# A weight ring of 20 slots in place of 18, each slot over the work region filled when its last reader is done

## The chip, the core and the metric

The kernel runs on one core of a Trainium2 chip. The metric is the device time of one execution in microseconds (us); lower is better. PE is the matrix engine, DVE the vector engine, ACT the scalar engine, POOL the general one, SP the engine whose queue issues most loads. 16 DMA engines serve the core.

## What is computed

Two layers of a model over 256 prompt tokens and 32 sample tokens (8 sequences of 4), D = 1024, all in 32-bit floats. Layer 0 has the even mixer (attention with forget gates, with paged keys and values for the samples, beside a gated delta rule), layer 1 the odd mixer (a gated product along chunks). Behind each mixer stands a mixture of 32 experts, of which each token takes two of one group:

```python
for layer in range(DEPTH):
    hp, hs = rms_norm(xp, norm_mix[layer]), rms_norm(xs, norm_mix[layer])
    ...                                    # even_mixer or odd_mixer gives mp, ms
    xp, xs = xp + mp, xs + ms
    xp = xp + hier_moe(rms_norm(xp, norm_ffn[layer]), *mprm)
    xs = xs + hier_moe(rms_norm(xs, norm_ffn[layer]), *mprm)

def hier_moe(h, w_rg, w_re, w_gate, w_up, w_down):
    ...                                    # group by argmax, two experts in it, softmax weights: gates
    act = silu(hg) * hu * gates[..., None] # hg, hu: h times w_gate[e], w_up[e], 1024 x 256 each
    return einsum('nlef,efd->nld', act, w_down)
```

The outputs are the rows behind the last norm, the new keys, values and gates, and the states; among these the samples' delta states (`delta_sample`, 2 MB).

## The kernel before

**The expert stage.** The experts are worked through in 8 turns (NQ) of 4 experts (QE). In a turn q, PE gathers the rows of its experts (`gather`, L1382, a product with a selection `pl`), multiplies them by gates and ups (`gate_up`, L1396; in turn 0 and 7 `gate_part`, L1415), transposes the activations (`act_turn`, L1436), multiplies by the downs (`down`, L1449; `down_last` in three parts, L1466) and adds the rows back in the next turn (`out_rows`, L1498 and L1507). ACT takes the silu (L2028, into `sg`), copies the transposes (L2033, into `avT`) and half of the products (L2041, into `ysb`), and a part of the gathered rows (`rows_in`, L2019, into `xgT`); DVE does the other parts (L2633, L2710, L2732), the additions to x (L2641, L2647), and in turn 0 the rare swap of a crowded expert (`swap`, L2573 to L2593, which ends with `meta_rdy`). The general case, in which an expert has more rows than fit, is a loop behind a branch that every engine takes at turn SPLIT = NQ - 2 = 6; it isn't entered with these inputs.

**The weights.** A unit is a gate, an up or a down of one expert, 1 MB. A layer has 96 units; unit u goes into slot u % RSLOTS of a ring, by one DMA on SP's queue (L487). `first_loads` issues the units from RSLOTS on, each when the unit that was in its slot before has been read (`first_free`: `part_ps` for the four gates of turn 0, then `gu_ps` and `dn_ps`). The ups and downs of the last turn come in pieces (L532, L526). Slots 0 to 7 (SLOTS) also hold the weights of the two mixers, one after another. Slots 8 and up lie over the work region of the mixers (`wk(offset)`: slot 8 + offset // 2048): in the even mixer for instance `S0`, the sample states, lies in slots 8 and 9, and in the odd mixer `vrow` in 8 to 10, `urow` in 11 to 13, the norm's weights in 14 and 15, `uT` from 17 on. Behind the ring lie 5240 columns that hold the router's and the expert stage's own tiles (`rt`, `pwT`, `spb`, `av`, `avT`, `ysb`, `cnt`).

**The order on SP's queue.** SP works strictly in order. At the end of a mixer it loads units 0 to 7, each as soon as the mixer's weights in its slot have been read (`even_used`, `odd_used`), then it waits for the end of the mixer and for all stores, and loads the others:

```python
sp.wait_ge(s.x_new, 6 * layer + 3)
sp.wait_ge(s.out_misc, 16 * (13 + layer))
for u in range(SLOTS, RSLOTS):
    moe_load(layer, 0, u)
first_loads(layer)
```

`x_new` counts the additions of the mixer's output to x (L2502, L2507), `out_misc` the stores, that of the samples' states (L1998, issued on ACT's queue when `dl_su` is 8) among them. The first expert stage is followed by the loads of the odd mixer's first 8 weights (`odd_first`), the second by the last norm's weight (`nfw`, slot 12).

**The router.** Before a stage PE transposes x in 8 pieces k (`transpose_k`, L812), ACT and DVE copy them to `hT`, and PE adds the product of each piece with the router's weights (L1340) two pieces behind the transposes; then come the choice of experts on DVE and the first gather.

## Time and profile before

| | |
|---|---|
| runs shown | 1065.19, 1061.83 and 1065.3 us, median 1065.19 us |
| profiled execution | 1060.95 us, its span 1059.0 us |
| busy in the span | PE 90%, PE's weight loads 54%, DVE 40%, ACT 22%, POOL 8% |
| matrix engine's granted clock | 0.972 of full speed in the mean |
| DMA | 292.63 MB, 276 GB/s in the mean; SP's queue 267.63 MB of it |

The span runs from the first to the last instruction; the execution's own time is 1.95 us longer. A share of busy time is a mean over stages with different limits: what sets the length of a stage is read from the waits in it and from what its DMA does meanwhile. The two expert stages lie at about 365 to 602 us and 813 to 1050 us.

### The profile page before, as it was taken

The numbers are of one execution on the slowest core, as the hardware profiler recorded it, in microseconds if no ns is written. First come the engines' busy times: TensorE is split into PE (matmuls) and PEld (weight loads), VectorE is DVE, ScalarE is ACT, GpSimd is POOL, SyncE is SP. The second block draws the span as 40 slices with busy tenths as digits, with TensorE's granted clock in tenths as the row PEclk, the third lists the DMA queues.
The fourth block names the chain that finished last, engine by engine and source line by source line (L and its number), as shares of the span: only waits on it lengthen the run. The fifth ranks groups of instructions, "written<-read, shape, count | busy, mean of one in ns | idle before, by whom it ended". The sixth has DMA issues, their size and how long they took to land.

```text
span 1059.0 us, 18436 instructions
## 1 busy us (share of the span) xinstructions
PE 957.5 (90%) x6934; PEld 576.6 (54%) x6934; DVE 424.1 (40%) x1105; ACT 237.8 (22%) x513; POOL 88.5 (8%) x199
## 2 busy tenths in 40 slices
PE   8999989899989999977788899999999999777885
PEld 7777767586884374533453444444444755333532
DVE  3733455465744346322534200252002553224343
ACT  3321136354201141110110311331002411010102
POOL 6333242140000000000000000000000000000000
PEclk9999999999979999988999999999999999899999
DMA  9951178795602599999999964443335899999995
GB/s 288 254 172 37 42 244 261 268 355 214 225 1 83 183 384 414 420 421 421 420 419 414 352 233 159 159 159 119 130 119 185 358 417 420 421 421 421 417 414 207
DMA packets 93391, 292.63 MB, mean 276 GB/s; under 512 B 16355, under 2 KB 56859, under 8 KB 66382
## 3 DMA queue, kind: packets, MB, share of 16 engines
q1 hardware_dynamic: 78836, 267.63, 66.1%
q0 software_dynamic: 5152, 17.05, 5.1%
q10 hardware_dynamic: 9306, 6.67, 2.0%
q8 instruction: 59, 0.97, 0.4%
q14 instruction: 38, 0.31, 0.1%
HBM read 286.17 MB, written 5.16 MB: 275 GB/s over the span
## 4 chain that ended last, share of the span: by engine, by line
PE 72%; DMA 15%; DVE 5%; SPq 3%; issue 3%; ACT 2%; ACTq 0%; DVEq 0%
DMA arena<-in_moe_w_up 13%; PE ps L1659 10%; PE ps L914 10%; PE ps L1396 8%; PE ps L1382 5%; PE ps L1749 5%; PE ps L1028 3%; PE ps L838 2%; DMA arena<-in_moe_w_down 2%; PE ps L1449 2%; PE ps L1041 2%; PE ps L829 2%; PE ps L1415 1%; PE ps L858 1%; PE ps L1652 1%
## 5 line engine op out<-in xcount | busy, mean ns | idle before, releaser
L1396 PE MATMUL ps<-arena,hT 128*32 128x512 f32 x768 | 95.6, 655 | 33.5 <-DMA arena<-in_moe_w_up 33.5
L1659 PE MATMUL ps<-arena,hT 128*128 128x512 f32 x256 | 111.0, 593 | 0.0
L914 PE MATMUL ps<-hT,arena 128*128 128x288 f32 x448 | 110.0, 407 | 0.0
L1382 PE MATMUL ps<-lvl,htok 128*128 128x128 f32 (+1 forms) x768 | 97.2, 284 | 14.0 <-issue 7.1
L1382 PEld LDWEIGHTS ps<-lvl,htok 128*128 128x128 f32 x768 | 91.9, 194 | 23.2 <-issue 17.7
L914 PEld LDWEIGHTS ps<-hT,arena 128*128 128x128 f32 x448 | 84.6, 190 | 23.5 <-issue 0.5
L1659 PEld LDWEIGHTS ps<-arena,hT 128*128 128x128 f32 x256 | 48.3, 190 | 59.7 <-issue 59.4
L1396 PEld LDWEIGHTS ps<-arena,hT 128*32 128x32 f32 x768 | 27.8, 119 | 96.1 <-issue 96.1
L1507 PE MATMUL ps<-arena 128*128 128x512 f32 x112 | 55.2, 618 | 3.8 <-DVE x L2641 3.8
L2633 DVE TENSOR_SCALAR hT<-ps,nw 128x128 f32<-128x128 f32 (+1 forms) x64 | 22.6, 354 | 75.9 <-PE ps L1382 75.8
L1449 PE MATMUL ps<-arena 128*32 128x512 f32 x448 | 51.0, 595 | 1.3 <-ACT arena L2033 1.3
L1749 PE MATMUL ps<-arena 128*128 128x512 f32 x112 | 49.2, 592 | 0.0
L2710 DVE TENSOR_TENSOR arena<-ps,lfp 128x256 f32<-128x256 f32 x16 | 6.8, 423 | 97.1 <-ACT lfp L2028 97.1
L2019 ACT ACTIVATE hT<-ps,nw 128x128 f32<-128x128 f32 (+1 forms) x64 | 23.7, 371 | 94.8 <-PE ps L1382 94.8
L2028 ACT ACTIVATE lfp<-ps 128x256 f32<-128x256 f32 x16 | 6.1, 384 | 168.9 <-PE ps L1396 138.0
L779 POOL DMA_DIRECT2D arena<-in_cache_v x64 | 33.8, 528 | 82.9 <-PE ps L1117 35.7
L757 POOL DMA_DIRECT2D lfp<-in_cache_logf x64 | 34.5, 539 | 61.2 <-issue 61.2
L1507 PEld LDWEIGHTS ps<-arena 128*128 128x128 f32 x112 | 18.9, 188 | 34.2 <-DVE x L2641 15.0
L2647 DVE TENSOR_TENSOR x<-x,ps 128x512 f32<-128x512 f32 x56 | 36.0, 684 | 2.7 <-PE ps L1507 2.3
L1749 PEld LDWEIGHTS ps<-arena 128*128 128x128 f32 x112 | 20.7, 190 | 23.4 <-issue 23.4
L1028 PE MATMUL ps<-ident,arena 128*128 128x128 f32 x256 | 32.2, 276 | 1.1 <-DVE hT L2304 1.0
L2732 DVE COPY arena<-ps 128x512 f32<-128x512 f32 x14 | 9.7, 692 | 53.3 <-PE ps L1449 53.3
(495 smaller groups left out, 1303.0 us busy)
## 6 DMA issues: line engine op xcount, KB each, us to landing
arena<-in_moe_w_gate SPq DMA_DIRECT2D x64, 1024.0 KB, 20.6
arena<-in_moe_w_up SPq DMA_DIRECT2D x56, 1024.0 KB, 20.9
arena<-in_moe_w_down SPq DMA_DIRECT2D x56, 1024.0 KB, 21.4
arena<-in_cache_k SPq DMA_DIRECT2D x64, 256.0 KB, 4.0
arena<-in_cache_v POOLq DMA_DIRECT2D x64, 256.0 KB, 3.9
arena<-in_w_in_odd SPq DMA_DIRECT2D x16, 1024.0 KB, 10.5
arena<-in_w_in_even SPq DMA_DIRECT2D x14, 1024.0 KB, 9.1
arena<-in_moe_w_up SPq DMA_DIRECT2D x16, 512.0 KB, 9.0
```

The costliest lines, as they stand in the source:

```text
L757: pool.dma_start(lfp[:, grp, pg, bass.ds(bl * 8, 8)], cl[bass.ds(page, 1)].rearrange("a r h -> r (a h)")).then_inc(s.bias_pages, 16)
L779: pool.dma_start(vquad[gi:P:4, qd, bl].rearrange("p j c -> p (j c)"), cvp[bass.ds(page, 1)].rearrange("a (p j) h d -> (a p) (j h d)", j=4))\
L914: last = mm(ps[:, c % 4, 0:T], w[:, k, P * (c % 2):P * (c % 2 + 1)], hT[:, k, :], start=k == 0, stop=k == KD - 1)
L1028: last = tr(ps[:, kt_bank(n), P * c:P * (c + 1)], kbuf[t % 4][:, n % 4, P * c:P * (c + 1)], ident[:, :])
L1382: last = mm(ps[:, row_bank(k), 0:w], htok[:, i, P * k:P * (k + 1)], pl[:, i, 0:w], start=i == 0, stop=i == 2)
L1396: last = mm(ps[EC * j:EC * (j + 1), q % 2, :], xgT[q % 2][:, k, EC * j:EC * (j + 1)], ring[:, sl:sl + 2, DE * k:DE * (k + 1)], start=k == ...
L1449: last = mm(ps[EC * j:EC * (j + 1), 3 + hf, :], avT[:, q % 2, f, EC * j:EC * (j + 1)], w[:, f, 512 * hf:512 * (hf + 1)], start=f == 0, sto ...
L1507: mm(ps[:, row_bank(j), :], pwT[:, q % 2, P * i:P * (i + 1)], ysb[:, 512 * hf:512 * (hf + 1)], start=True, stop=True).then_inc(s.o_ps, 1)
L1659: last = mm(ps[:, bank, :], hT[:, k, P * i:P * (i + 1)], ring[:, oslot(2 * n):oslot(2 * n) + 2, QC * k:QC * (k + 1)], start=k == 0, stop=k ...
L1749: mm(ps[:, b, :], uT[:, c, P * (b // 2):P * (b // 2 + 1)], w[:, e, 512 * (b % 2):512 * (b % 2 + 1)], start=c == 0, stop=False)
L2019: A_(xgT[q % 2][:, k, 0:w], ps[:, row_bank(k), 0:w], ACT.Copy, scale=nw[:, n_, k:k + 1])\
L2647: V.tensor_tensor(xs, xs, ps[:, row_bank(j), :], ALU.add).then_inc(s.xadd, 1)
```

## The change

- RSLOTS is 20. The ring takes 4096 columns more, and the columns behind it shrink from 5240 to 1441: `spb`, `lgT` and one `pwT` stay there; `av`, `sg`, `avT`, `ysb`, `cnt` and the other `pwT` go to tiles that are idle in the expert stage, and `av`, `sg` and `avT` have one buffer in place of two. `rt` goes to the end of `hT`, under `xgT[1]`; what of it is needed later (`w1`, `w2`, `spq`) goes to `sm`, and ACT waits for `meta_rdy` before it writes `xgT[1]`.
- The slots over the work region are loaded by `fill_even` and `fill_odd`, each group when its last reader is done; 18 and 19 wait for the end of the mixer.
- The store of the samples' states has its own semaphore `s0_stored`; only slots 8 and 9, where they lie, wait for it.
- The branch is at turn SPLIT = 4.
- The router transposes two pieces and then multiplies two.
- Behind the first stage, SP loads the odd mixer's weights 0 to 3 when turn 6's downs have been read, and 4 to 7 when turn 7's gates and ups have been read.
- Some semaphores are merged (`fz_ln` and `dl_dtx` into `act_ln`, `rt_exp2` into `rl_sb`, `hot_dve` and `y_quarter` into `side_dve`).

The diff, cut to its core:

```diff
-MSLOTS, RSLOTS = 3 * QE, 18
+MSLOTS, RSLOTS = 3 * QE, 20
...
-        arena = sb("arena", [P, RSLOTS * UNIT + 5240])
+        arena = sb("arena", [P, RSLOTS * UNIT + 1441])
...
-        rt = wk(M, 3, 320)
-        pwT = wk(M + 1344, 2, T)
-        spb = wk(M + 1920, 4, T)
-        lgT = wk(M + 1920, 3 * P)
-        av = wk(M + 3072, 2, DE)
-        avT = wk(M + 3584, 2, FT, P)
-        ysb = wk(M + 4096, D)
-        cnt = wk(M + 5120, 112)
+        spb = wk(M, 4, T)
+        lgT = wk(M, 3 * P)
+        pwT = [wr[:, 0, :, :].rearrange("p k c -> p (k c)"), wk(M + 1152, T)]
+        av, sg = neg2, wsm[:, :, :].rearrange("p k c -> p (k c)")
+        ysb = [lfp[:, :, :, :].rearrange("p a b c -> p (a b c)"), cst[:, 1024:1536]]
+        cnt = cst[:, 320:432]
+        avT = cst[:, 432:432 + FT * P].rearrange("p (f c) -> p f c", f=FT)
         pw2 = cs27[:, :, :].rearrange("p c w -> p (c w)")[:, 0:T]
-        sg = lfp[:, :, :, :].rearrange("p a b c -> p (a b c)").rearrange("p (a b) -> p a b", a=2)
...
-        nfw = ring[:, 12, 0:D]
+        rt = xgf[:, KD * (P + EC) + 64:].rearrange("p (t c) -> p t c", t=3)
+        nfw = ring[:, 16, 0:D]
...
-        SPLIT = NQ - 2
+        SPLIT = NQ - 4
...
+
+            def fill_even():
+
+                def over_weights(*us):
+                    for u in us:
+                        even_used(EVEN_UNITS - SLOTS + (u - EVEN_UNITS) % SLOTS)
+                        moe_load(0, 0, u)
+
+                over_weights(2, 3, 4, 5)
+                sp.wait_ge(s.dl_oss_ps, 1)
+                sp.wait_ge(s.dl_vexp, NB)
+                for u in (14, 15, 16, 17):
+                    moe_load(0, 0, u)
+                over_weights(6, 7, 0)
+                sp.wait_ge(s.dl_su, 8)
+                for u in (10, 11, 12, 13):
+                    moe_load(0, 0, u)
+                over_weights(1)
+                sp.wait_ge(s.x_new, 3)
+                sp.wait_ge(s.out_misc, 16 * 12)
+                for u in range(18, RSLOTS):
+                    moe_load(0, 0, u)
+                sp.wait_ge(s.s0_stored, 16)
+                for u in (8, 9):
+                    moe_load(0, 0, u)
+
+            def fill_odd():
+
+                def over_weights(*us):
+                    for u in us:
+                        odd_used(ODD_UNITS - SLOTS + u)
+                        moe_load(1, 0, u)
+
+                sp.wait_ge(s.gm_sum, 6)
+                for u in (14, 15):
+                    moe_load(1, 0, u)
+                over_weights(0, 1, 2, 3)
+                moe_load(1, 0, 17)
+                over_weights(4)
+                sp.wait_ge(s.gm_m_ps, HC + 1)
+                moe_load(1, 0, 16)
+                sp.wait_ge(s.out_misc, 16 * 13)
+                for u in (8, 9, 10):
+                    moe_load(1, 0, u)
+                over_weights(5)
+                sp.wait_ge(s.gm_t_ps, NU)
+                for u in (11, 12, 13):
+                    moe_load(1, 0, u)
+                over_weights(6, 7)
+                sp.wait_ge(s.x_new, 9)
+                for u in range(18, RSLOTS):
+                    moe_load(1, 0, u)
 
             def first_loads(layer):
                 for u in range(RSLOTS, MOE_UNITS):
@@ -580,10 +636,7 @@
 
             def odd_first(r):
                 sp.wait_ge(s.gu_ps, past(0, r, NQ, NQ))
-                for j in (0, 1, 6, 7):
-                    odd_load(j)
-                sp.wait_ge(s.dn_ps, past(0, r, NQ, NQ))
-                for j in range(2, 6):
+                for j in range(SLOTS):
                     odd_load(j)
                 if layer == 0:
-                    for u in (2, 3, 4, 5, 6, 7, 0, 1):
-                        even_used(EVEN_UNITS - SLOTS + (u - EVEN_UNITS) % SLOTS)
-                        moe_load(0, 0, u)
+                    fill_even()
                 else:
-                    for u in range(SLOTS):
-                        odd_used(ODD_UNITS - SLOTS + u)
-                        moe_load(1, 0, u)
-                sp.wait_ge(s.x_new, 6 * layer + 3)
-                sp.wait_ge(s.out_misc, 16 * (13 + layer))
-                for u in range(SLOTS, RSLOTS):
-                    moe_load(layer, 0, u)
+                    fill_odd()
                 first_loads(layer)
                 with sp.If(more(sp, layer) > 0):
                     with sp.Fori(1, ROUNDS) as r:
@@ -665,11 +710,20 @@
                     else:
                         final_weights(ROUNDS - 1)
                 with sp.Else():
-                    for sl in range(MSLOTS):
+                    for sl in range(4):
                         wait_first(sp, layer, in_slot[sl][-1])
                         sp.sem_inc(s_w[sl], 16 * (ROUNDS - 1) * RL)
                     if layer == 0:
-                        odd_first(0)
+                        sp.wait_ge(s.dn_ps, past(0, 0, NQ, NQ - 1))
+                        for j in range(4):
+                            odd_load(j)
+                    for sl in range(4, MSLOTS):
+                        wait_first(sp, layer, in_slot[sl][-1])
+                        sp.sem_inc(s_w[sl], 16 * (ROUNDS - 1) * RL)
+                    if layer == 0:
+                        sp.wait_ge(s.gu_ps, past(0, 0, NQ, NQ))
+                        for j in range(4, SLOTS):
+                            odd_load(j)
                         skip_rounds(sp)
                     else:
...
-                for k in range(KD + 2):
-                    if k < KD:
-                        transpose_k(n, k, ROWS_FIRST[2:] if k < EARLY else ROWS_FIRST)
-                    if k >= 2:
-                        hT_copied(n, k - 2)
-                        last = mm(ps[0:36, 4, 0:T], wr[:, layer, k - 2, :], hT[:, k - 2, :], start=k == 2, stop=k == KD + 1)
+                for j in range(0, KD + 2, 2):
+                    for k in (j, j + 1):
+                        if k < KD:
+                            transpose_k(n, k, ROWS_FIRST[2:] if k < EARLY else ROWS_FIRST)
+                    for k in (j - 2, j - 1):
+                        if k >= 0:
+                            hT_copied(n, k)
+                            last = mm(ps[0:36, 4, 0:T], wr[:, layer, k, :], hT[:, k, :], start=k == 0, stop=k == KD - 1)
                 last.then_inc(s.rl_ps, 1)
...
+                            last = tr(ps[:, 2, P * f:P * (f + 1)], av[:, f::FT], ident[:, :])
                         last.then_inc(s.t_ps, 1)
...
-            act.dma_start(t["delta_sample"][0].rearrange("b h k v -> k (b h) v"), S0[:, :, :]).then_inc(s.out_misc, 16)
+            act.dma_start(t["delta_sample"][0].rearrange("b h k v -> k (b h) v"), S0[:, :, :]).then_inc(s.s0_stored, 16)
...
+                        if first and q == 1:
+                            act.wait_ge(s.meta_rdy, 2 * layer + 2)
                         for k in range(1, KD, 2):
                             W(s.g_ps, KD * NQ, KD * q + k + 1)
...
-                        if q >= 2:
-                            W(s.act, NQ, q - 1)
-                        A_(sg[:, q % 2], ps[:, q % 2, 0:DE], ACT.Silu).then_inc(s.silu, 1)
+                        if q:
+                            W(s.act, NQ, q)
+                        A_(sg, ps[:, q % 2, 0:DE], ACT.Silu).then_inc(s.silu, 1)
                         if first and q == X_TURN:
                             act.wait_ge(s.hot_ps, 4 * layer + 2)
...
```

## Rows read from the trace of the kernel before

**Rows 1.** Waits of PE (who waited for whom: us in total, times, longest).
```profile
PE ps L1396 <- DMA arena<-in_moe_w_up: 33.5, 8, 6.7
...
PE ps L1466 <- DMA arena<-in_moe_w_down: 3.8, 3, 2.1
```

**Rows 2.** Windows of 20 us (busy by engine, granted clock, DMA share, GB/s).
```profile
300.00:320.00 20.00, 17.80 (x220) 16.30 (x218) 8.35 (x20) 2.46 (x6) 0.00 (x0) 0.82 0.01 2
```

**Rows 3.** Timeline of PE, first expert stage (start, us, what, idle before).
```profile
434.53 7.08 PE L1396 MATMUL ps<-arena,hT 128*32 128x512 f32 x64 [0.31 <-DMA arena<-in_moe_w_up]
...
464.43 8.56 PE L1396 MATMUL ps<-arena,hT 128*32 128x512 f32 x64 [5.95 <-DMA arena<-in_moe_w_up]
...
494.28 9.00 PE L1396 MATMUL ps<-arena,hT 128*32 128x512 f32 x64 [6.70 <-DMA arena<-in_moe_w_up]
...
524.36 8.77 PE L1396 MATMUL ps<-arena,hT 128*32 128x512 f32 x64 [3.88 <-DMA arena<-in_moe_w_up]
...
551.32 2.25 PE L1382 MATMUL ps<-lvl,htok 128*128 128x128 f32 x18 [3.62 <-issue]
...
590.98 4.15 PE L1466 MATMUL ps<-arena 128*32 128x512 f32 x32 [2.09 <-DMA arena<-in_moe_w_down]
```

**Rows 4.** Timeline of PE, second expert stage.
```profile
912.75 9.68 PE L1396 MATMUL ps<-arena,hT 128*32 128x512 f32 x64 [5.99 <-DMA arena<-in_moe_w_up]
...
1039.19 1.92 PE L1466 MATMUL ps<-arena 128*32 128x512 f32 x16 [1.05 <-DMA arena<-in_moe_w_down]
```

**Rows 5.** Windows of 4 us at the stages' starts and the first one's end.
```profile
360.00:364.00 4.00, 4.00 (x10) 1.72 (x10) 1.65 (x3) 1.15 (x2) 0.00 (x0) 1.00 1.02 290
...
392.00:396.00 4.00, 4.00 (x56) 2.66 (x60) 2.02 (x9) 1.65 (x2) 0.00 (x0) 1.00 0.60 250
396.00:400.00 4.00, 4.00 (x68) 2.56 (x61) 3.21 (x21) 0.38 (x1) 0.00 (x0) 1.00 0.81 279
...
588.00:592.00 4.00, 1.53 (x10) 0.74 (x14) 0.33 (x1) 0.38 (x1) 0.00 (x0) 0.80 1.09 357
...
840.00:844.00 4.00, 4.00 (x56) 2.66 (x56) 1.96 (x9) 1.62 (x2) 0.00 (x0) 1.00 0.37 154
844.00:848.00 4.00, 4.00 (x67) 2.56 (x60) 3.22 (x22) 0.41 (x2) 0.00 (x0) 1.00 0.80 268
```

**Rows 6.** Timeline of the SP queue: issues of weight loads.
```profile
365.45 2.22 SPq L487 DMA_DIRECT2D arena<-in_moe_w_down  x4
...
395.75 0.33 SPq L487 DMA_DIRECT2D arena<-in_moe_w_gate  x1
...
575.68 15.45 SPq L526 DMA_DIRECT2D arena<-in_moe_w_down  x12
...
843.81 0.33 SPq L487 DMA_DIRECT2D arena<-in_moe_w_gate  x1
```

**Rows 7.** Timeline at the end of the even mixer, ACT's queue and DVE.
```profile
355.87 0.40 ACTq L1998 DMA_DIRECT2D out_delta_sample<-arena  x1
...
361.30 0.69 DVE L2507 TENSOR_TENSOR x<-x,ps 128x512 f32<-128x512 f32 x1 [1.03 <-PE ps L858]
...
364.74 0.69 DVE L2507 TENSOR_TENSOR x<-x,ps 128x512 f32<-128x512 f32 x1 [1.03 <-PE ps L858]
```

**Rows 8.** Timeline of PE in the router (and of transposes alone).
```profile
368.22 0.60 PE L812 MATMUL ps<-ident,x 128*128 128x128 f32 x3
...
369.35 0.60 PE L812 MATMUL ps<-ident,x 128*128 128x128 f32 x3
...
372.15 1.65 PE L1340 MATMUL ps<-hT,wr 128*36 128x288 f32 x6
...
602.40 2.96 PE L822 MATMUL ps<-ident,x 128*128 128x128 f32 x24
```

**Rows 9.** Timeline of DVE and ACT in turn 0.
```profile
399.04 0.19 DVE L2593 TENSOR_TENSOR arena<-arena 128x48 f32<-128x48 f32 x1
...
401.90 0.36 ACT L2019 ACTIVATE hT<-ps,nw 128x128 f32<-128x128 f32 x1
```

97 lines of the change are left out of this document (50 added, 47 removed).

## Prediction

> **What bounds the kernel now.** I read the page first, its 40 slices above all: in the two expert stages the DMA row stands at 9 throughout, and PE's is no higher than elsewhere. So I asked for the waits of PE. The longest is that of the gate-and-up products (L1396) for `moe_w_up`, 33.5 us in 8 waits; the waits for `moe_w_down` are 3.8 us [rows 1]. PE waits little, but a stage is bound by what paces it, and that is read from the timeline of PE: its product of turn 3 starts at 464.43 us after 5.95 us of idleness, that of turn 4 at 494.28 us, that of turn 5 at 524.36 us [rows 3]. The distance is 29.8 and 30.1 us, and PE's own work in a turn is some 23 us (464.43 to 487.58 us, where the wait of 6.70 us begins). 12 units of 1 MB are loaded in a turn, so one unit costs (524.36 - 464.43) / 24 = 2.50 us. The second stage goes the same way: waits of 5.99 us at 912.75 us and its like [rows 4].
>
> When does this stream start? Windows of 4 us show it: the DMA share falls to 0.60 at 392 to 396 us and 0.81 in the next window, and to 0.37 and 0.80 at 840 to 848 us [rows 5]. There all 18 slots are full and the stream stands still until the first gate products free slots 0 to 3: the queue issues again at 395.75 and 843.81 us [rows 6]. The DMA is idle 2.4 us in the first case (0.40 x 4 + 0.19 x 4) and 3.3 us in the second. From there 96 - 18 = 78 units go at 2.50 us each, and the last pieces land when PE has nothing else left: it waits 2.09 us at 590.98 us and 1.05 us at 1039.19 us [rows 3, 4]. Before the stages DMA stands idle: 2 GB/s from 300 to 320 us [rows 2].
>
> So the length of an expert stage is the moment of the first free slot, plus (96 - ring slots) units at 2.50 us, plus a tail.
>
> **The ring of 20 slots.** 76 units are left at the first free slot in place of 78, if the ring is full by then. That is 2 x 2.50 = 5.0 us in each stage, 10.0 us in all. Does a new stall eat it? Turn 2's product waits only 0.31 us now [rows 3]; with units 5.0 us earlier it is PE that paces turn 2 (ready at 434.22 us), the next arrival is at 464.43 - 5.0 = 459.4 us, and PE is ready at 458.2 us: it waits again from turn 3 on. While PE lags, the stream must not run out of slots: at 434.53 us the products of turns 0 and 1 have read their 24 units, so the slots for all units up to 43 are free, and at 2.50 us a unit from 397 us on only 20 + 15 = 35 have landed. It doesn't.
>
> **The fill as readers finish.** Without it a ring of 20 would be full 5.0 us later than now, at 394.4 + 5.0 us, and the gain would be only the idle DMA time, 2.4 + 3.3 = 5.7 us. With 18 slots the fill by itself would be worth nothing, as the ring is full before the first free slot as it is. Together: in layer 0, slots 14 to 17 can go at about 327 us, 10 to 13 at 355.9 us (the sample states' last addition; their store is issued then [rows 7]), 18 and 19 at 365.4 us, 8 and 9 when the store has landed. From 355.9 us on, some 9 MB of loads and 2 MB of store are left, 11.5 x 2.5 = 29 us: full by 385 us, 11 us before the first free slot. In layer 1 all but four loads are issued before 813 us, so the ring is full by some 827 us, and 843.81 us is far. Each fill is issued by the SP queue in order; behind its waits stand only other fills, and none of these is wanted before 385 us. In the fills' time the mixer's PE and DVE work goes on beside more traffic. DVE's addition of the output product takes 0.69 us at 361.30 us, where the DMA share is 1.02 [rows 5, 7], and 0.69 us at 364.74 us, behind it, so I cost the overlap at nothing.
>
> **The own semaphore for the state store.** The store is issued at 355.87 us, and the first load after x_new and the store was issued at 365.45 us; DVE's addition that gives x_new ends at 365.43 us [rows 6, 7]. So the store took at most 9.6 us, and SP waited for x_new. Now it shares the engines with four loads issued at the same moment: if it came last of all 11.5 MB it would land at 385 us, and units 8 and 9 at 390 us; PE reads them in turn 0's down products, behind ACT's copy at 401.90 us [rows 9]. Cost nothing. The Trainium skill ("DMA: Bandwidth & Descriptors", section "Issuing engines are not separate DMA queues") says that DMAs of different issuing engines run on the same 16 engines and interleave; by that the store is slowed by the loads, which is what the bound above allows for, and the sum stays the same.
>
> **The branch at turn 4.** Now it stands before turn 6: PE is idle 3.62 us at 547.7 us, and its first product of the next turn starts at 551.32 us [rows 3]. At turn 4 the same time lies within the wait of 6.70 us for weights. PE then comes 5.0 + 3.6 = 8.6 us earlier to the last pieces, at 580.3 us, but they land only 5.0 us earlier, at 586.0 us: the branch's time turns into a wait and is worth nothing (3.6 us a stage if the pieces came in time). The single buffers of `av`, `sg` and `avT` cost nothing either: PE's order has the reader of turn q - 1 before the writer of turn q. ACT's new wait for `meta_rdy` before it overwrites `rt` is over at 399.23 us, and ACT's first such copy starts at 401.90 us [rows 9].
>
> **The router's loop in pairs.** One step (three transposes, one product) starts every 1.13 us [rows 8]. By themselves three transposes take 2.96 / 8 = 0.37 us and a product 1.65 / 3 = 0.55 us [rows 8], so two changes of kind cost 0.21 us a step. Halving them saves 0.1 us in each of 5 to 8 steps: 0.5 us in each layer, 1.0 in all; the bounds are 0 and 1.0 a layer. This does count, as the whole stage hangs on the first free slot.
>
> **PE's clock in the tail.** Where PE had waited some 6 us, the next product took 8.56, 9.00 and 9.68 us in place of 7.07 us [rows 3, 4], so such a wait costs 1.5 to 2.6 us. In the stream this is inside the next wait. In the tail it isn't: PE's idle time there grows from 2.1 to 5.7 us, in pieces (for the second halves of the ups, then for the downs). Bounds 0 and 2.6 us for each layer; as pieces are shorter than the waits of those rows, and layer 0 already has 0.80 in that window [rows 5], I take 1.0 each, 2.0 in all. The Trainium skill ("TensorE: Matmul & The Clock Gate", section "HAM oscillation — how this bites in real kernels") warns that a wait for DMA puts the array back to half speed; the rows agree, 1.5 to 2.6 us each. By the rule with the rows' full price the sum would be 3.2 us worse. This is the rule that speaks most against hiding the branch in a wait.
>
> **Loads of the odd weights.** They are issued behind the last pieces, whose issues begin at 575.68 us and last 15.45 us [rows 6], and will be issued earlier, still behind them on the same queue. If they shared the engines with the pieces instead, four loads could push those back by up to 10 us in layer 0; the order of the queue is my reason to cost it at nothing.
>
> **Sum:** -10.0 - 1.0 + 2.0 = -9.0 us. The profiled execution took 1060.95 us (span 1059.0 us), so 1052.0 by it; the median of the runs shown is 4.2 us above it, 1065.19 us, and gives 1056.2 us. I take 1056.
>
> **Rivals.** (a) More is gained: if the last pieces come late because SP issues them late, not because the engines are full, they follow PE (whose products free the slots), and the branch's 3.6 us count twice as well: -16, 1049 us. For it: the pieces' issues last 15.45 us. Against it: the share of 1.09 at 588 to 592 us [rows 5]. (b) The clock: every wait in the tails at the full 2.6 us, and no gain in the router: -4.8 us, 1060 us. For it stand the rows of turns 3 to 5; against it that the waits are shorter. (c) The change doesn't do what it says: the ring isn't full at the first free slot, because a fill is released late. Then the gain is the 5.7 us of idle DMA less 1.0 us, 1060 us. Against it is the margin of 11 us. (d) Slower: SP stands in order at the wait for the state store, and units 8, 9 and the whole stream stand behind it. Each us by which the store lands after 395.75 us is lost in layer 0. It decides from 406 us on, that is 50 us after its issue (9.0 us gained are then given back); for 1071 us it would be 65 us. Against it: at most 9.6 us now [rows 6, 7].
>
> **Chances.** The forecast 0.66, with its own range of 1053 (-12.0: router at 1.0, tails at 0) to 1060 (-4.8: router at 0, tails at 2.6). (a) 0.10, (b) 0.11, (c) 0.08, (d) 0.05. The range of 1049 to 1062 takes in (a) and (b), (c) with the spread of the runs shown (3.5 us), and leaves (d) and the edges of the others out. About 0.5%, 5.3 us, is what a measurement can tell from no change, so faster is below 1059.9 us: 0.63 of the forecast, 0.10 of (a), 0.05 of (b), 0.03 of (c), 0.81; slower is (d), 0.05; the rest, 0.14, is the same.
>
> **What will show it.** The share of DMA before the first free slot falls to 0 for some 10 us in layer 0 and more in layer 1; the distance from the first free slot to the start of turn 3's, 4's and 5's product is 5 us shorter, the distance of 30 us between them is the same; no idle time of 3.6 us before turn 6's gather; a wait of some 5 us in all in the last turn. The prediction is wrong if the share falls below 1 between turns 1 and 6, if the first free slot itself moves by more than 1 us, or if the tail is longer by more than 2.6 us.

## The result and the profile after

The changed kernel took 1051.9 us (median of 4 runs, 1050.17 to 1054.88), the kernel before in the same comparison 1063.55 us (4 runs, 1061.83 to 1065.3): ratio 0.9893, interval 0.9861 to 0.9925. The forecast was 1056 us against the 1065.19 us shown then, -9.2 us; the runs say -11.65 us.

The profiled pair shows less: 1060.95 us before and 1054.88 us after, the slowest of its four runs. So the sum of the prediction is checked stage by stage. A stage's clock starts at its first router transpose, and is read at the first down product of turn 7 and at the end of the stage (the x transposes of the odd mixer, and the end of the span). What lies between the first down product of turn 7 and the end of the stage is called the tail. All columns but the first are distances, worked out from the starts in the timeline of PE.

| profiled execution, us | first router transpose | stage 1 to downs of turn 7 | stage 1 whole | odd mixer | stage 2 to downs of turn 7 | stage 2 whole | both stages |
|---|---|---|---|---|---|---|---|
| before | 364.5 | 226.5 | 237.9 | 209.9 | 226.9 | 246.7 | 484.5 |
| after | 366.4 | 219.9 | 232.9 | 213.0 | 220.5 | 241.1 | 474.0 |

The stages lost 10.6 us (forecast 9.0): -6.6 and -6.3 us up to the last downs, +1.5 and +0.8 us in the tails. 4.9 us came back outside the stages: 1.8 us ahead of the first router, 3.1 us in the odd mixer. No run shows that either is the change's doing. The first router transpose starts anywhere from 362.68 us (spin_short) to 368.81 us (again) in the profiled executions; in late_fill, which fills nothing early, it starts at 368.10 us, and in store_on_sp, which fills early, at 364.69 us. So it isn't shown that the traffic of the early fill slows the even mixer; its spread of 6 us is larger than most terms of this document, and is left out by reading distances inside the stages.

Waits of PE, after (answers to [rows 1]):

```profile
PE ps L1452 <- DMA arena<-in_moe_w_up: 28.1, 6, 8.1
PE ps L1471 <- DMA arena<-in_moe_w_up: 7.0, 3, 3.1
...
PE ps L1522 <- DMA arena<-in_moe_w_down: 4.6, 2, 2.3
```

Timeline of PE, after (start, us, what, idle before; answers to [rows 3, 4, 8]):

```profile
369.38 0.92 PE L866 MATMUL ps<-ident,x 128*128 128x128 f32 x6
370.24 1.16 PE L1396 MATMUL ps<-hT,wr 128*36 128x288 f32 x4
...
434.67 7.07 PE L1452 MATMUL ps<-arena,hT 128*32 128x512 f32 x64
...
459.81 7.07 PE L1452 MATMUL ps<-arena,hT 128*32 128x512 f32 x64 [1.18 <-DMA arena<-in_moe_w_up]
...
489.58 8.87 PE L1452 MATMUL ps<-arena,hT 128*32 128x512 f32 x64 [8.11 <-DMA arena<-in_moe_w_up]
...
520.92 8.57 PE L1452 MATMUL ps<-arena,hT 128*32 128x512 f32 x64 [5.27 <-DMA arena<-in_moe_w_up]
...
553.93 7.07 PE L1452 MATMUL ps<-arena,hT 128*32 128x512 f32 x64
...
580.53 1.93 PE L1471 MATMUL ps<-arena,hT 128*32 128x256 f32 x32 [2.68 <-DMA arena<-in_moe_w_up]
...
586.25 5.35 PE L1522 MATMUL ps<-arena,cst 128*32 128x512 f32 x32 [2.31 <-DMA arena<-in_moe_w_down]
...
599.20 2.94 PE L876 MATMUL ps<-ident,x 128*128 128x128 f32 x24
...
668.11 30.73 PE L1715 MATMUL ps<-arena,hT 128*128 128x512 f32 x64
...
1032.73 4.37 PE L1522 MATMUL ps<-arena,cst 128*32 128x512 f32 x32 [2.29 <-DMA arena<-in_moe_w_down]
```

The reader is to see four things. Turn 3's product now waits 1.18 us, turn 4's 8.11 us: it holds the branch's 3.6 us and what is left of the wait of 6.70 us. The idle 3.62 us at the start of turn 6's gather [rows 3] is gone, and in its place stand 2.68 and 2.31 us in the last turn: 5.0 us, as forecast. The first downs (586.25 us) take 5.35 us, in the second stage 4.37 us; the same 32 matmuls took 4.15 us before [rows 3], and 32 such matmuls take 3.64 us in a turn that doesn't wait for DMA (563.14 us). Last, the odd mixer's third block of projections (668.11 us) takes 30.73 us, where it took 27.73 us in the kernel before.

Windows of after, the first of 20 us, the others of 4 us (answers to [rows 2, 5]; granted clock, DMA share and GB/s stand last):

```profile
300.00:320.00 20.00, 18.29 (x216) 17.01 (x215) 7.69 (x18) 1.75 (x4) 1.18 (x1) 0.78 0.01 2
...
384.00:388.00 4.00, 4.00 (x34) 3.28 (x32) 3.07 (x16) 0.37 (x1) 0.00 (x0) 1.00 0.41 117
388.00:392.00 4.00, 4.00 (x42) 2.70 (x42) 0.35 (x1) 0.42 (x2) 0.00 (x0) 1.00 0.99 414
392.00:396.00 4.00, 4.00 (x52) 2.46 (x48) 1.50 (x6) 1.48 (x3) 0.00 (x0) 1.00 0.01 2
396.00:400.00 4.00, 4.00 (x71) 2.36 (x64) 3.44 (x23) 0.75 (x2) 0.00 (x0) 1.00 0.65 223
...
584.00:588.00 4.00, 1.75 (x12) 0.53 (x16) 0.00 (x0) 0.35 (x1) 0.00 (x0) 0.68 1.10 354
588.00:592.00 4.00, 4.00 (x32) 1.39 (x24) 0.35 (x1) 0.60 (x1) 0.00 (x0) 0.50 0.98 320
...
668.00:672.00 4.00, 4.00 (x9) 1.91 (x8) 3.57 (x16) 0.00 (x0) 0.00 (x0) 0.50 1.06 353
...
824.00:828.00 4.00, 4.00 (x21) 3.54 (x19) 2.51 (x13) 3.97 (x4) 0.00 (x0) 1.00 0.00 0
```

The ring of the first stage is full at some 392 us, not at 385 us, with a hole in the traffic at 384 to 388 us. (SP issues its first load of a freed slot at 396.27 us; in the queue's rows below it is merged with the issues before it. From there the gate-and-up products of turns 3, 4 and 5 start 5.1, 5.2 and 4.0 us earlier than before and the last downs 5.3 us; the distance between turns is 29.8 and 31.3 us.) What held it up is seen in the queues of SP and ACT, after (answers to [rows 6, 7]):

```profile
357.63 0.43 ACTq L2054 DMA_DIRECT2D out_delta_sample<-arena  x1
...
357.63 0.80 SPq L491 DMA_DIRECT2D arena<-in_moe_w_down  x2
...
367.64 0.43 SPq L491 DMA_DIRECT2D arena<-in_moe_w_up  x1
385.25 13.15 SPq L491 DMA_DIRECT2D arena<-in_moe_w_down  x6
...
566.53 19.96 SPq L530 DMA_DIRECT2D arena<-in_moe_w_down  x12
587.97 19.30 SPq L491 DMA_DIRECT2D arena<-in_w_in_odd  x8
```

After 367.64 us SP stands at `s0_stored`, and issues units 8 and 9 only at 385.25 us: the state store took 27.6 us from its issue, where at most 9.6 us were read before [rows 6, 7]. It landed last of all, at the moment that the prediction worked out as the worst case (385 us). In these 27.6 us ACT's queue moved 2.10 MB in 4112 packets and SP's queue 7.34 MB in 1011 packets.

Timeline of DVE and ACT, after (answers to [rows 7, 9]):

```profile
366.55 0.69 DVE L2565 TENSOR_TENSOR x<-x,ps 128x512 f32<-128x512 f32 x1 [1.03 <-PE ps L912]
...
399.56 0.19 DVE L2651 TENSOR_TENSOR sm<-sm,hT 128x48 f32<-128x48 f32 x1
...
402.42 0.76 ACT L2077 ACTIVATE hT<-ps,nw 128x128 f32<-128x128 f32 x2
```

DVE's additions take 0.69 us beside the loads, as before. DVE's last write that `meta_rdy` guards ends at 399.75 us, and ACT's first copy behind that wait starts at 402.42 us, so the wait costs nothing.

### The profile page after: what moved, and what is told of

Read it like the earlier page. It is cut to its first block, busy times and chain, and to the rows that moved or that the text cites. A ratio compares the mean times of both kernels' runs of the same rounds, so it can differ in the third digit from the quotient of the medians.

```text
span 1053.3 us, 18440 instructions
## 1 busy us (share of the span) xinstructions
PE 957.4 (91%) x6934; PEld 578.1 (55%) x6934; DVE 424.0 (40%) x1105; ACT 237.5 (23%) x513; POOL 88.9 (8%) x199
## 4 chain that ended last, share of the span: by engine, by line
PE 70%; DMA 12%; SPq 7%; DVE 6%; ACT 2%; issue 2%; ACTq 0%; DVEq 0%
PE ps L1715 11%; PE ps L968 10%; DMA arena<-in_moe_w_up 9%; PE ps L1438 6%; PE ps L1805 5%; PE ps L1452 4%; SPq L491 4%; PE ps L1082 3%; DMA arena<-in_moe_w_down 2%; PE ps L892 2%; PE ps L1505 2%; PE ps L1095 2%; PE ps L883 2%; PE ps L1563 1%; PE ps L1471 1%
## 5 line engine op out<-in xcount | busy, mean ns | idle before, releaser
L1452 PE MATMUL ps<-arena,hT 128*32 128x512 f32 x768 | 90.3, 624 | 28.1 <-DMA arena<-in_moe_w_up 28.1
L1715 PE MATMUL ps<-arena,hT 128*128 128x512 f32 x256 | 114.0, 606 | 0.0
L1438 PEld LDWEIGHTS ps<-lvl,htok 128*128 128x128 f32 x768 | 90.2, 191 | 15.5 <-issue 10.6
L1505 PE MATMUL ps<-arena,cst 128*32 128x512 f32 x448 | 51.0, 595 | 1.4 <-ACT cst L2091 1.4
L1805 PE MATMUL ps<-arena 128*128 128x512 f32 x112 | 49.2, 592 | 0.0
L2086 ACT ACTIVATE wsm<-ps 128x256 f32<-128x256 f32 x16 | 6.2, 385 | 166.4 <-PE ps L1452 127.2
L2768 DVE TENSOR_TENSOR neg<-ps,wsm 128x256 f32<-128x256 f32 x16 | 6.8, 423 | 84.1 <-ACT wsm L2086 84.1
L1471 PE MATMUL ps<-arena,hT 128*32 128x256 f32 x512 | 31.2, 382 | 7.6 <-DMA arena<-in_moe_w_up 7.0
L1805 PEld LDWEIGHTS ps<-arena 128*128 128x128 f32 x112 | 20.7, 190 | 23.4 <-issue 23.4
L1082 PEld LDWEIGHTS ps<-ident,arena 128*128 128x128 f32 x256 | 29.0, 145 | 4.1 <-issue 3.0
L2790 DVE COPY cst<-ps 128x512 f32<-128x512 f32 x14 | 9.7, 692 | 53.3 <-PE ps L1505 53.3
```

The source lines that it names most:

```text
L1082: last = tr(ps[:, kt_bank(n), P * c:P * (c + 1)], kbuf[t % 4][:, n % 4, P * c:P * (c + 1)], ident[:, :])
L1438: last = mm(ps[:, row_bank(k), 0:w], htok[:, i, P * k:P * (k + 1)], pl[:, i, 0:w], start=i == 0, stop=i == 2)
L1452: last = mm(ps[EC * j:EC * (j + 1), q % 2, :], xgT[q % 2][:, k, EC * j:EC * (j + 1)], ring[:, sl:sl + 2, DE * k:DE * (k + 1)], start=k == ...
L1471: last = mm(ps[EC * j:EC * (j + 1), q % 2, DE * part:DE * (part + 1)], xgT[q % 2][:, k, EC * j:EC * (j + 1)], ring[:, sl, DE * k:DE * (k + ...
L1505: last = mm(ps[EC * j:EC * (j + 1), 3 + hf, :], avT[:, f, EC * j:EC * (j + 1)], w[:, f, 512 * hf:512 * (hf + 1)], start=f == 0, stop=f == ...
L1715: last = mm(ps[:, bank, :], hT[:, k, P * i:P * (i + 1)], ring[:, oslot(2 * n):oslot(2 * n) + 2, QC * k:QC * (k + 1)], start=k == 0, stop=k ...
```

## The experiments

Ratios are against the kernel before in the same job, which was run 11 to 17 times in each (medians 1067.13, 1064.07, 1069.8 and 1063.46 us in jobs 1 to 4). Each profile is of one execution, so its distances have no interval; two executions of the same program differ by up to 0.4 us in a stage (after and again) or 1.9 us (before and before_again). "To the downs" is the distance from the first router transpose to the first down product of turn 7, in stage 1 / stage 2.

| run | job | median us (lowest to highest) | ratio, interval | to the downs | both stages | odd mixer |
|---|---|---|---|---|---|---|
| again | 1 | 1051.55 (1048.4 to 1054.04) | 0.9847, 0.9814 to 0.9881 | 220.1 / 220.3 | 473.7 | 209.9 |
| late_fill | 1 | 1054.2 (1051.65 to 1056.98) | 0.9875, 0.9841 to 0.9908 | 222.5 / 222.7 | 477.4 | 209.9 |
| ring18 | 1 | 1059.82 (1057.79 to 1062.45) | 0.9938, 0.9913 to 0.9964 | 224.9 / 225.3 | 483.0 | 209.9 |
| split6 | 1 | 1052.18 (1051.04 to 1053.75) | 0.9859, 0.9825 to 0.9892 | 220.7 / 221.2 | 472.4 | 211.6 |
| unpaired | 2 | 1051.56 (1049.88 to 1052.79) | 0.9874, 0.9851 to 0.9896 | 221.4 / 221.7 | 474.7 | 209.9 |
| split4_alone | 2 | 1063.1 (1060.75 to 1065.5) | 0.9982, 0.9963 to 1.0 | 226.3 / 226.8 | 486.2 | 209.9 |
| spin_tail | 2 | 1052.59 (1051.56 to 1053.72) | 0.9885, 0.9863 to 0.9906 | 222.0 / 222.2 | 473.3 | 211.6 |
| store_on_sp | 2 | 1051.46 (1049.99 to 1052.59) | 0.9876, 0.9852 to 0.99 | 220.2 / 220.3 | 473.7 | 209.9 |
| spin_short | 3 | 1049.4 (1048.25 to 1052.99) | 0.9838, 0.9801 to 0.9874 | 220.4 / 221.4 | 472.4 | 211.6 |
| spin_short_mid_store | 3 | 1049.63 (1048.53 to 1051.2) | 0.9828, 0.9793 to 0.9863 | 220.2 / 220.5 | 471.3 | 209.9 |
| odd_late | 3 | 1049.95 (1047.33 to 1051.69) | 0.9828, 0.9781 to 0.9875 | 220.2 / 220.7 | 474.1 | 209.9 |
| before_again | 4 | 1064.77 (1059.61 to 1071.91) | 1.0003, 0.9978 to 1.0028 | 227.1 / 228.0 | 485.9 | 217.7 |

**again**: the changed kernel, unchanged.

> The changed kernel once more, beside the variants. Theory (the stream): two units fewer behind the first free slot in each expert stage, 10.0 us, and 1.0 us from the router: 11 us less than before, ratio 0.990. Rival (the profiled pair alone is to be believed, 1060.95 and 1054.88 us): 6 us less, ratio 0.994.

The stages' 473.7 us repeat the 474.0 us; the odd mixer takes 209.9 us again, so its 3.1 us in the first profile belong to that execution. The total fits neither number on record: it is 15.6 us below before, where 11 and 6 us were named. 9 of the 16 executions of before in this job took over 1066 us (see before_again); against the other seven, whose median is 1063.72 us, it is 12.2 us.

**late_fill**: all first fills stand behind `x_new` and the stores.

```diff
-                    fill_even()
+                    for u in (2, 3, 4, 5, 6, 7, 0, 1):
+                        even_used(EVEN_UNITS - SLOTS + (u - EVEN_UNITS) % SLOTS)
+                        moe_load(0, 0, u)
...
+                sp.wait_ge(s.x_new, 6 * layer + 3)
+                sp.wait_ge(s.out_misc, 16 * (12 + layer))
+                sp.wait_ge(s.s0_stored, 16)
+                for u in range(SLOTS, RSLOTS):
+                    moe_load(layer, 0, u)
```

> The changed kernel with its ring of 20, but all slots over the work region are loaded behind x_new and the stores, as before the change. Theory (the stream is all that counts): the ring is full 5.0 us later than in the kernel before, so only the idle DMA time of the kernel before, 2.4 + 3.3 = 5.7 us, is gained, and 1 us in the router: 6.7 us less than before, 4.3 us more than the changed kernel; no idle DMA at the start of the stages. Rival (two units fewer are worth 10 us whenever the ring is filled): as the changed kernel. Rival (the fill's traffic slows the mixers): faster than the changed kernel.

To the downs it is 3.9 and 4.2 us shorter than before. Less the router's 1.3 and 1.4 us (below) that is 2.6 and 2.8 us for the idle time of the DMA engines, against 2.4 and 3.3 us read from [rows 5]. In the total it is 2.65 us slower than again, where 4.3 us were expected. Windows of 4 us of late_fill show that the stream has no gap at the first free slots:

```profile
392.00:396.00 4.00, 4.00 (x42) 2.40 (x41) 0.70 (x2) 0.37 (x1) 0.00 (x0) 1.00 1.01 418
396.00:400.00 4.00, 4.00 (x73) 2.51 (x76) 3.17 (x19) 1.65 (x2) 0.00 (x0) 1.00 1.01 422
840.00:844.00 4.00, 4.00 (x68) 2.60 (x68) 2.74 (x17) 1.65 (x2) 0.00 (x0) 1.00 1.00 416
```

**ring18**: the changed kernel with 18 slots.

```diff
-MSLOTS, RSLOTS = 3 * QE, 20
+MSLOTS, RSLOTS = 3 * QE, 18
...
-    arena = sb("arena", [P, RSLOTS * UNIT + 1441])
+    arena = sb("arena", [P, 20 * UNIT + 1441])
```

(`nfw` lies in slot 12 again, and the odd weights are loaded in the order of before.)

> The changed kernel with 18 slots in place of 20 (all else of it kept: the early fill, the branch at turn 4, the router in pairs; the order of the odd mixer's first weights is that of before). Theory: the ring was full in time before, so the early fill is worth nothing by itself; 1 us from the router, so 1 us less than before and 10 us more than the changed kernel. Rival (filling as readers finish pays by itself): clearly less than before, by 5 us or more.

To the downs -1.5 and -1.6 us against before: what the router gives, and little else. The total says more, -7.3 us where -1.0 us was expected, and taken by itself it would speak for the recorded rival (5 us or more). Against the executions of before of up to 1066 us it is still -3.9 us, of which the stages hold 1.6 us (484.5 and 483.0 us); the rest is not in the stages, and no run assigns it. Windows of 4 us of ring18 show the early fill, 18 units, done before 388 us, and DMA standing still behind it:

```profile
388.00:392.00 4.00, 4.00 (x43) 2.54 (x42) 0.77 (x3) 0.74 (x2) 0.00 (x0) 1.00 0.02 4
392.00:396.00 4.00, 4.00 (x42) 2.67 (x42) 0.40 (x3) 0.38 (x2) 0.00 (x0) 1.00 0.00 0
396.00:400.00 4.00, 4.00 (x76) 2.37 (x77) 3.72 (x21) 1.64 (x2) 0.00 (x0) 1.00 0.41 115
```

Early fill by itself is worth nothing in a stage, two slots alone 2.4 and 2.6 us (late_fill less ring18), both together 4.9 and 5.0 us (again less ring18): 5.0 us were forecast. That is the stream law, measured with either part taken away.

**split6**: the branch at turn 6 in the changed kernel. **split4_alone**: the branch at turn 4 in the kernel before.

```diff
-SPLIT = NQ - 4
+SPLIT = NQ - 2
```

That is split6; split4_alone has the opposite edit in the kernel before.

> The changed kernel with its branch at turn 6 again. Theory: the 3.5 us of the branch lie ahead of a wait for the last pieces, so the time is that of the changed kernel, within 1 us, and PE's waits in turn 7 are shorter by about 3.5 us in each stage. Rival (the last turns are paced by PE): 7 us more than the changed kernel.

> The kernel before, with the branch at turn 4 and nothing else. Theory: the 3.6 and 3.5 us turn into waits for the last pieces, which land when they did: no difference to before (within 1.5 us), PE's wait for the downs of the last turn grows from 2.1 to over 5 us. Rival (the end of the stage follows PE): 7 us less than before.

split6 takes the same time as again (1052.18 and 1051.55 us). Its PE has its idle 3.54 us back ahead of turn 6 and reaches the last pieces without the long waits. Timeline of PE, split6:

```profile
547.95 7.22 PE L1438 MATMUL ps<-lvl,htok 128*128 128x128 f32 x48 [3.54 <-issue]
...
588.30 1.92 PE L1522 MATMUL ps<-arena,cst 128*32 128x512 f32 x16 [1.72 <-DMA arena<-in_moe_w_down]
```

Its stages are even 1.3 us shorter than those of again (472.4 and 473.7 us): its tails are 10.7 and 19.8 us in place of 12.9 and 20.4 us, and the granted clock is 1.00 from 588 to 600 us and from 1032 to 1044 us, where again has 0.50 at 588 to 592 us and 0.62 at 1032 to 1036 us. In split4_alone the way to the downs is that of before to 0.2 us, and the stages together are 1.7 us longer (486.2 and 484.5 us), all of it in the tail of stage 2. (PE's wait for the last downs is 2.33 us there, not over 5 us; the other 2.52 us come earlier, at the second halves of the ups.) So the branch's place is worth nothing up to the last downs, as expected, and with the branch hidden in a wait the tails lose 1.3 and 1.7 us of clock in these profiles: most of what the prediction put down as the clock's term. That is one profile each, and before and before_again differ by as much. What it is worth elsewhere comes with before_again.

**unpaired**: the router's products follow each piece of transposes again.

```diff
-                for j in range(0, KD + 2, 2):
-                    for k in (j, j + 1):
+                for k in range(KD + 2):
```

> The changed kernel with the router's loop one piece at a time, as before. Theory: the first free slot comes 0.5 us later in each layer, 1.0 us more than the changed kernel in all (bounds 0 and 2). Rival (the loop is hidden behind ACT's and DVE's copies): no difference, and the distance from the last addition of x_new to the product of turn 1 (44.8 us before, 44.2 us in the changed kernel) stays at 44.2 us.

Timeline of PE in the router, unpaired:

```profile
369.63 0.60 PE L866 MATMUL ps<-ident,x 128*128 128x128 f32 x3
370.16 0.68 PE L1394 MATMUL ps<-hT,wr 128*36 128x288 f32 x2
370.76 0.60 PE L866 MATMUL ps<-ident,x 128*128 128x128 f32 x3
```

A step starts every 1.13 us, as before; after the change two steps take 1.95 us (369.38 us to the next transposes at 371.33 us). To the downs unpaired is 1.3 and 1.4 us longer than again: this is the router's term, not 0.5 us. The rival (no difference) falls with it. The totals don't show it (1051.56 us, and store_on_sp of the same job, which has the pairs, 1051.46 us). The tail of stage 1 is 11.8 us in unpaired and 12.9 us in again, that of stage 2 19.8 and 20.4 us: PE arrives later, waits less and loses less of its clock. Over the whole stages the pairs are therefore worth only 1.0 us (474.7 and 473.7 us).

**spin_tail**, **spin_short**: 8 dummy matmuls (products whose results nobody uses) ahead of the wait for the second halves of the ups in turn 7, and 8 ahead of the first `down_last`; spin_short has 5 and 4. **spin_short_mid_store** has 2 more ahead of two waits of the odd mixer, and the store as in store_on_sp.

```diff
+                            spin(0, 8)
                             pe.wait_ge(s.wu_half, 16 * QE * (layer + 1))
...
+                            spin(0, 8)
                             down_last(0)
```

> The changed kernel, with 8 products of constants (no use is made of their results) ahead of the wait for the second halves of the ups and 8 ahead of the wait for the downs in turn 7 of both layers: about 1.8 us each, which fit into the waits of 2.7 to 3.1 and 2.3 us. Theory (PE's clock falls in these waits and makes the tail longer: the first down products took 5.35 us in place of 4.15, the granted clock was 0.50 at 588 to 592 us): the clock stays at 1.0, the down products of the last turn take 3.6 us, and 1.5 to 3 us less than the changed kernel in all. Rival (the clock in the tail doesn't matter, or the products come in the way): the same or up to 1 us more.

> The changed kernel with the filling products of the run before made shorter: there each call was 2 instructions of 0.23 us, so that 8 calls took 3.7 us and PE came 2 us late (first downs at 588.35 us in place of some 586.2). Here 5 calls (2.3 us) stand ahead of the wait for the second halves (2.7 to 3.1 us) and 4 (1.8 us) ahead of the wait for the downs (2.3 us). Theory (the clock falls in the waits of turn 7): from the stage's first transpose to its end 230 and 239 us (in the changed kernel 232.9 and 241.1 us, with the long fillers 232.1 and 241.2), so 3 to 4 us less than the changed kernel. Rival (the tail's length hangs on something else): the distance from the first transpose to the first downs is that of the changed kernel, 219.9 and 220.5 us, and the tail behind it isn't shorter than 13.0 and 20.6 us.

> As spin_short, and two more edits: 2 filling calls (0.9 us) in each of the two waits of 0.97 us of PE for DVE in the middle of the odd mixer (where PE's clock fell in one of the profiles: 12.27 us for what took 9.28 us in the others), and the store of the sample states on SP's queue. Theory: as spin_short in the stages; the odd mixer takes 209.9 us from the transposes of x to the router in every run (it took 213.0 us in one, 211.6 us in two, 209.9 us in the others), so some 0.5 us less in the mean; the fastest of all, some 1048 us. Rival: as spin_short, within the noise.

spin_tail held the clock, but a block of 8 takes 3.7 us (each dummy is two instructions of 0.23 us) and PE came 2 us late to the pieces: the tails are 10.0 and 19.0 us in place of 12.9 and 20.4 us, and the 2 us are lost ahead of them; the 1.5 to 3 us expected didn't come. The short version, windows of 4 us of spin_short:

```profile
580.00:584.00 4.00, 3.14 (x22) 2.06 (x26) 0.23 (x1) 0.38 (x1) 0.00 (x0) 1.00 1.08 353
584.00:588.00 4.00, 3.36 (x34) 1.25 (x27) 0.42 (x1) 0.60 (x1) 0.00 (x0) 1.00 0.92 311
```

The granted clock stays at 1.00 (2.4 GHz) in the tail of stage 1, where after had 0.68 at 584 and 0.50 (1.2 GHz) at 588 us, and the stage takes 231.3 us in place of 233.0 us (again). In stage 2 the clock stays at 1.00 too and the tail is 0.7 us shorter (19.8 us), but the last downs start 1.1 us later than in again, and the stage gains nothing (241.1 us). The recorded 230 and 239 us were not reached, nor did the rival hold. So the clock in the tail of stage 1 costs some 1.7 us, shown in one profile by taking it away, and split6 without dummies has the same (231.35 us). In the total this isn't seen: 1049.4 us, and odd_late of the same job, without dummies, 1049.95 us. spin_short_mid_store (1049.63 us) is like spin_short, as its rival said. No version measurably beats the changed kernel.

**store_on_sp**: the state store on SP's queue, ahead of the loads of units 10 to 13.

```diff
                 sp.wait_ge(s.dl_su, 8)
+                sp.dma_start(t["delta_sample"][0].rearrange("b h k v -> k (b h) v"), S0[:, :, :]).then_inc(s.s0_stored, 16)
                 for u in (10, 11, 12, 13):
...
-            act.wait_ge(s.dl_su, 8)
-            act.dma_start(t["delta_sample"][0].rearrange("b h k v -> k (b h) v"), S0[:, :, :]).then_inc(s.s0_stored, 16)
```

> The changed kernel, with the store of the sample states issued on SP's queue ahead of the loads of slots 10 to 13, in place of ACT's queue. Theory (on its own queue the store gets a small part of the engines beside the loads: it landed 27.6 us after its issue, and units 8 and 9 are issued only at 385.25 us; in the queue of the loads it is served in its turn): it lands within 12 us, units 8 and 9 are issued at x_new (some 367 us), the ring is full by about 387 us in place of 392 us; the time is the same, as the first slot is freed at 397 us. Rival (the fill is only just in time and costs something): 1 us or more less than the changed kernel.

Timeline of the SP queue, store_on_sp:

```profile
355.97 0.40 SPq L573 DMA_DIRECT2D out_delta_sample<-arena  x1
356.41 6.67 SPq L491 DMA_DIRECT2D arena<-in_moe_w_down  x2
...
366.46 30.52 SPq L491 DMA_DIRECT2D arena<-in_moe_w_down  x6
```

The store took at most 10.5 us, and units 8 and 9 were issued at 366.46 us, 19 us earlier than after. The ring is full before 388 us, as expected, and the time is the same: after, too, the ring is full before the first free slot.

**before_again**: the kernel before, unchanged. **odd_late**: the changed kernel with the odd mixer's first 8 weights in the order of before.

```diff
-                        sp.wait_ge(s.dn_ps, past(0, 0, NQ, NQ - 1))
-                        for j in range(4):
-                            odd_load(j)
...
-                        for j in range(4, SLOTS):
-                            odd_load(j)
+                        odd_first(0)
                         skip_rounds(sp)
```

> The kernel before once more, for its profile. Beside the variants its own times ran from 1061 to 1074 us, while the same kernel with the branch at turn 4 (split4_alone) stayed within 1060.8 to 1065.5 us and the changed kernel within 1048.4 to 1054.9 us. Theory (the branch at turn 6 takes longer in some executions, and PE then comes late to the last pieces): if the profiled execution is one of over 1066 us, the idle time of PE ahead of turn 6's gather is well over 3.6 us in a stage, and the stage is longer by what exceeds the wait of 2.1 us for the downs. Rival (PE's clock in the mixers is what differs): the stages take 237.9 and 246.7 us as before, and the mixers are longer. Where the execution is one of some 1062 us, it tells nothing of this, and only gives the stages once more.

> The changed kernel, with the odd mixer's first 8 weights issued as in the kernel before: all behind the landing of the last turn's first pieces, four behind turn 7's gates and ups and four behind its downs. Theory (they are wanted late and come behind the pieces on the same queue): no difference within 1 us, PE's first projection starts without a wait. Rival (issued early they share the engines with the last pieces): here the first downs of layer 0 come earlier after the stage's start than 219.9 us, by 1 us or more, and the kernel is faster by as much. Rival (the early issue closes a gap that matters): 1 us or more slower, with a wait of PE ahead of the projections.

These two go after a gain that the stages don't hold. Of all 67 executions of the kernel before in the four jobs 30 took over 1066 us, up to 1073.87 us; no execution of a kernel with 20 slots took over 1056.98 us. The profiled execution of before_again is such a one, 1071.91 us. Its stages take 485.9 us, 1.4 us more than before; the odd mixer takes 217.7 us in place of 209.9 us. The theory on record falls: PE's idle time ahead of turn 6 is 3.60 us, no longer than before. The rival was right in that the mixer is longer, and wrong in the cause: there is a wait in it. Timeline of PE and the SP queue, before_again:

```profile
554.02 7.22 PE L1382 MATMUL ps<-lvl,htok 128*128 128x128 f32 x48 [3.60 <-issue]
...
606.45 13.93 PE L1659 MATMUL ps<-arena,hT 128*128 128x512 f32 x32
...
625.31 16.55 PE L1659 MATMUL ps<-arena,hT 128*128 128x512 f32 x32 [4.93 <-DMA arena<-in_w_in_odd]
...
579.47 15.23 SPq L526 DMA_DIRECT2D arena<-in_moe_w_down  x12
596.72 15.71 SPq L487 DMA_DIRECT2D arena<-in_w_in_odd  x7
```

PE waits 4.93 us for a weight and then loses 2.6 us to a lower clock (0.50 at 624 to 628 us; 16.55 and 13.93 us for the same 32 matmuls). Read backwards: SP needs 15.23 us to issue the 12 last pieces, 1.27 us each (15.45 us in the first profile of before, which I take for SP's own pace); it starts when PE's turn 6 frees slots, and PE stands 3.60 us at the branch right ahead of turn 6. Here PE's turn 6 is 2.0 us late (its gate-and-up product starts 199.3 us after the stage's first transpose, 197.3 us in the first profile), 1.0 us of it from turn 5's product, which took 9.74 us in place of 8.77 us; the issue of the pieces is 2.0 us and that of the odd weights 1.8 us late by the same measure. The odd weights are issued behind the pieces, here 9.7 us ahead of the first product that reads them (606.45 - 596.72 us). In the first profile of before it is 12.0 us (605.19 and 593.15 us), and there is no wait. After the change it is 14.0 us (601.98 and 587.97 us), in odd_late 13.4 us. The distance isn't the whole story: the weight that PE waits for is wanted 13.9 us behind that first product, and the last of the eight issues took 9.12 us here and 3.16 us in the first profile.

Kernels with one of the two changes keep clear of it too: none of 12 executions of split4_alone took over 1065.5 us, where 6 of 17 of before in the same job took over 1066 us, and none of 11 of ring18 over 1062.45 us; these have the branch at turn 4 and 18 slots. split6, with 20 slots and the branch at turn 6, has none of 6 over 1053.75 us. odd_late, with the order of before, has none over 1051.69 us. In split4_alone the issues of the last pieces start at 572.76 us and take 18.48 us: as I read it, SP is waiting for slots there and is no longer the pace. So the earlier issue of the odd weights isn't needed with 20 slots; that the branch's place or the slots do it fits the times of all of these. How they do it is not shown: in their profiled executions the odd weights are issued 12.1 us (split4_alone), 12.4 us (ring18) and 11.7 us (split6) ahead of use, no more than in the first profile of before. That SP's slack takes up a late turn 6 there is my reading, and that every execution over 1066 us met this wait is argued from one profile.

## Why the prediction was right

**The stream law (-5.0 us a stage): right.** again less ring18 is 4.9 and 5.0 us, with slots and fill together; the parts alone give what they should. In windows of 8 us of after the share of DMA is 1.00 or more from turn 1 to turn 6, as the sign asked.

**The late fill reasoning (5.7 us): right**, 2.6 and 2.8 us measured.

**The router (-0.5 us a layer): the term that was mis-sized.** It measured 1.3 and 1.4 us. Two old steps took 2.26 us, two paired ones take 1.95 us: 0.31 us, 1.24 us in the four pairs. My sum took 0.1 us a step where it is 0.155 us, and 5 to 8 steps where it is all 8. The bound of 1.0 us a layer was too low as well. That the pairs come to 1.0 us over the whole stages, the number of the sum, is luck: the tails give the rest back. By the prediction's own sign, "wrong if the first free slot itself moves by more than 1 us", the slot did move: SP issues its first load of a freed slot 29.9 us after the first router transpose (396.27 and 366.35 us; late_fill the same), before 31.2 us. By that sign this term failed, while the total stayed in its range.

**PE's clock in the tails (+2.0 us): right in sum, uneven.** +1.5 and +0.8 us. The Trainium skill ("TensorE: Matmul & The Clock Gate", section "HAM oscillation — how this bites in real kernels") says that a wait for DMA can put the array back to half clock, so that the work behind it starts cold; the rows agree (0.50 at 588 us, behind waits of 2.68 and 2.31 us), and spin_short, which fills such waits with matmuls, kept 1.00 there.

**The branch (0 in the stages): right up to the last downs.** Where it went is seen as 8.11 us in turn 4 and 5.0 us of waits in turn 7. split6 confirms it from the other side, and adds that the +2.0 us of the line above are for the most part its price: with the branch at turn 6 the stages are 1.3 us shorter.

**The fill's time: right in price, wrong in margin.** The ring was full at some 392 us in place of 385 us. The step "Now it shares the engines with four loads" named the worst case and I set the margin without it. The store was slow by its place: on ACT's queue beside SP's loads 27.6 us, on SP's queue at most 10.5 us. The Trainium skill ("DMA: Bandwidth & Descriptors", section "Queues, rings and completion order") says that a DMA engine takes turns between the queues that have work for it, one packet at a time. With packets of 510 B on ACT's queue and 7.3 KB on SP's (2.10 MB in 4112, 7.34 MB in 1011) that would give the store the smaller part of the bytes, which it got; but it moved four packets for each one of SP's, so plain turns between the packets that the profile counts don't give the share, and no run here separates the causes. Of the 11 us of margin 4.3 were left (392 and 396.27 us), so rival (c) was nearer than its 0.08 said.

**Odd weights (0): incomplete.** They don't disturb the last pieces, as forecast (again and odd_late both 220 us to the downs). But the step looked only at whom they disturb, not at who waits for them. The profile of before showed 12.0 us from issue to use and no wait, and I took it for the rule. A term for that is missing from the sum; as far as the one profile shows, a part of the gain outside the stages comes from there.

**Rivals.** (a) fell: the pieces' issues start 9.15 us earlier after the change (566.53 and 575.68 us), stretch to 19.96 us and still land with the stream. (b) fell with the router (no gain there was its condition) and with the tails (2.3 us, not 5.2 us). (d) was the nearest miss of mechanism: SP did stand at the store, 17 us, and was let go 11 us before the first free slot.

**The sum:** -10.6 us in the stages against -9.0 us forecast. By its terms the difference is the router: -2.7 us measured for -1.0 us, beside -10.2 us for the stream and +2.3 us for the tails. The total has more: -11.65 us in the first comparison, though no execution of before took over 1065.3 us in it, and -15.6 us in job 1 (1067.13 and 1051.55 us), of which 3.4 us are the executions of before over 1066 us. That these are late in the odd mixer is argued from one profile. The 1.0 to 1.6 us that are left beyond the stages stay open.

## What to carry to other kernels

A weight stream that bounds a stage is shortened by units landed before the first slot comes free, and by an earlier first free slot; more slots alone give only the idle time of the DMA engines (late_fill), and early issue alone gives nothing (ring18). Time saved on a waiting engine turns into longer waits, and the waits take part of it back by the clock. A profile without a wait doesn't show that a transfer comes in time in every execution: look at the spread of the runs, and ask which transfer could be late.

## What the runs showed of the hardware that was not expected

- The same store of 2 MB took 27.6 us on ACT's queue beside loads on SP's queue, and at most 10.5 us when issued on SP's queue ahead of the loads.
- PE's clock in the mixers differs between executions of the same instructions: in after it was 0.50 at 668 to 672 us and cost 3.0 us (30.73 in place of 27.73 us), in again it didn't; the odd mixer took 209.9 to 213.0 us in the profiles in which it never waits for a weight. Dummy matmuls at its waits gave 209.9 us in the one profile taken, which shows nothing, as eight of the twelve others without a wait have it too. Before the first router the executions differ by as much as 6 us.
- Transposes and products of the router cost PE 0.31 us more for two pieces when they alternate piece by piece than in pairs (2.26 and 1.95 us), though no row shows idle time for it.
